# A two-block transformer kernel: token-major products take 512 weight columns at a time instead of 256

## The reference, cut to what matters

```python
h = rms_norm(x, mix_norm_g)
proj = h @ w_in                       # 512 x 1024 times 1024 x 5888
z_a, q, k, v, gate_logits = jnp.split(proj, [1536, 2304, 3072, 3840], axis=-1)
y_a = chunked_spatial_gating(gelu(z_a), ...)   # u = columns 0..767, v-part = 768..1535
...
y_b = dilated_mixture_attention(q, k, v)       # v: 3 groups of 4 heads x 64 = 3 x 256 columns
```

## Time and profile before

| | |
|---|---|
| median of 3 runs | 1986.85 us |
| the profiled execution | 1987.81 us, of which the span of the trace 1986.0 us |
| TensorE matmuls busy | 1874.4 us, 94% of the span, 9685 instructions |
| TensorE weight loads busy | 1373.3 us, 69%, 9691 instructions |
| VectorE, ScalarE, GpSimd busy | 983.6 us, 657.0 us, 85.3 us |
| mean granted TensorE clock | 0.977 of full speed |

### The profile page before, as it was taken

How to read it: one execution, slowest core, us unless ns; L and a number is a source line. 1 busy time by engine, 2 the same in 40 slices (tenths; PEclk the granted TensorE clock), 3 DMA queues, 4 the chain that set the end, 5 groups by cost and what they waited for, 6 DMA issues and landing times.

```text
span 1986.0 us, 23349 instructions
## 1 busy us (share of the span) xinstructions
PE 1874.4 (94%) x9685; PEld 1373.3 (69%) x9691; DVE 983.6 (50%) x1620; ACT 657.0 (33%) x1134; POOL 85.3 (4%) x70
## 2 busy tenths in 40 slices
PE   6989999999999699999999799999898999999998
PEld 4877777788878434344433289898677788888886
DVE  4888877843552422231322254525565556636643
ACT  4445544532332301020110144223545443222333
POOL 0200000000000000000000000002130200000000
PEclk9999999999999799999999999999898999999999
DMA  9332333252343499999999932252211332233221
GB/s 323 120 111 92 121 92 96 88 188 94 104 182 115 152 419 421 421 421 422 420 421 421 395 107 82 89 171 64 64 43 64 129 99 90 75 128 106 66 93 43
DMA packets 176539, 355.13 MB, mean 179 GB/s; under 512 B 7122, under 2 KB 148530, under 8 KB 151090
## 3 DMA queue, kind: packets, MB, share of 16 engines
q1 hardware_dynamic: 172688, 338.85, 46.3%
q10 hardware_dynamic: 3458, 14.50, 2.0%
q0 software_dynamic: 288, 0.30, 0.1%
HBM read 345.53 MB, written 8.39 MB: 178 GB/s over the span
## 4 chain that ended last, share of the span: by engine, by line
PE 77%; DVE 10%; ACT 5%; DMA 4%; issue 2%; POOL 2%; SPq 0%; ACTq 0%; DVEq 0%; POOLq 0%
PE ps L487 74%; PE ps L490 2%; DMA rx<-in_w_exp_up 1%; DMA rx<-in_w_exp_down 1%; DVE small L2122 1%; ACT M L1238 1%; POOL X L2790 1%; DVE wsp0l L1877 1%; DVE wsq1l L1877 1%; DMA md<-in_w_mod 1%; DVE X L1886 1%; DVE k2l L1877 1%; ACT KR L1238 1%; POOL tb L2790 1%; POOL MH L2790 1%
## 5 line engine op out<-in xcount | busy, mean ns | idle before, releaser
L487 PE MATMUL ps<-H,wsq1h 128*128 128x512 f32 x640 | 200.2, 394 | 4.7 <-DVE wsq1l L1877 2.7
L487 PE MATMUL ps<-H,wsq0h 128*128 128x512 f32 x608 | 191.0, 395 | 0.2 <-DVE wsq0l L1877 0.2
L487 PE MATMUL ps<-rx,XE 128*64 128x512 f32 x752 | 176.7, 600 | 2.9 <-DMA rx<-in_w_exp_up 2.2
L487 PE MATMUL ps<-H,wsp1h 128*128 128x512 f32 x544 | 173.8, 401 | 1.4 <-DVE wsp1l L1877 1.4
L487 PEld LDWEIGHTS ps<-H,wsq1h 128*128 128x128 f32 x640 | 119.7, 189 | 30.4 <-issue 6.1
L487 PEld LDWEIGHTS ps<-H,wsq0h 128*128 128x128 f32 x608 | 114.5, 190 | 25.4 <-issue 2.3
L487 PE MATMUL ps<-H,wsq1l 128*128 128x512 f32 x320 | 125.2, 391 | 0.0
L487 PE MATMUL ps<-H,wsp0h 128*128 128x512 f32 x368 | 121.4, 408 | 2.1 <-ACT H L1238 2.1
L1877 DVE TENSOR_TENSOR wsq1l<-ring,wsq1h 128x1024 fp32r<-128x1024 f32 (+2 forms) x72 | 82.9, 1191 | 78.0 <-ACT wsq1h L1238 77.9
L487 PE MATMUL ps<-H,wsq0l 128*128 128x512 f32 x304 | 119.0, 391 | 0.0
L487 PEld LDWEIGHTS ps<-H,wsp1h 128*128 128x128 f32 x544 | 100.6, 192 | 22.2 <-issue 3.5
(11 more groups left out here) (378 smaller groups left out, 3576.0 us busy)
## 6 DMA issues: line engine op xcount, KB each, us to landing
rx<-in_w_exp_gate SPq DMA_DIRECT2D x49, 1024.0 KB, 17.2
rx<-in_w_exp_down SPq DMA_DIRECT2D x46, 1024.0 KB, 20.7
rx<-in_w_exp_up SPq DMA_DIRECT2D x45, 1024.0 KB, 19.4
ring<-in_w_in SPq DMA_DIRECT2D x39, 1024.0 KB, 5.3
ring<-in_w_up SPq DMA_DIRECT2D x20, 1024.0 KB, 5.1
ring<-in_w_exp_up SPq DMA_DIRECT2D x19, 1024.0 KB, 20.6
ring<-in_w_mod SPq DMA_DIRECT2D x18, 1024.0 KB, 6.9
ring<-in_w_exp_down SPq DMA_DIRECT2D x18, 1024.0 KB, 19.3
```

Of the source, the lines that this page charges most:

```text
L487: return pe.e.matmul(o, l, r, start=start, stop=stop, skip_group_check=True)
```

## The change

`lin_n` now works on a pair of slabs, each of 4 chunks of 128 rows by 512 columns (also 1 MB). It goes through the four token tiles with the first slab (h = 0) and again with the second (h = 1), so four banks are open at once, and each is complete, with 512 columns, only in the second round. The 768 columns of `v2` and the 256 columns of the first attention group, 1024 in all, become two such pairs; the second takes its columns from two places in `w_in_2`, so each of its slabs is loaded by two transfers. The 512 columns of attention groups 2 and 3 become one pair `av`, with tokens r, r+4, .... ScalarE empties a bank of the second pair in two steps (gelu into `vg`, scaled copy into `va`), one of `av` in a single 512-column step. `va` moves to a place of its own, since it is now written while `vg` is still wanted, and `vr`, `pT2`, `mk2`, `idb2` and `pp` shift with it. The eight steps of `first_norm` are spread over four slabs instead of three.

```diff
-    for n in range(3):
-        piece(("v2", n), w_in2, 0, 8, 768 + 256 * n)
+    for h in range(2):
+        piece(("v2", 0, h), w_in2, 4 * h, 4, 768, 512)
+    for h in range(2):
+        slab(("v2", 1, h), [(0, 256, rows(w_in2, 4 * h, 4, 1280, 256)), (256, 512, rows(w_in2, 4 * h, 4, 3072, 256))], 4, 512)
...
-    for n in range(3):
-        piece(("av", n), w_in2, 0, 8, 3072 + 256 * n)
+    for h in range(2):
+        piece(("av", 0, h), w_in2, 4 * h, 4, 3328, 512)
...
+        def lin_n(key, hh, hl, toks, frees):
+
+            for h in range(2):
+                s = slabs[key + (h,)]
+                wh, wl = hi_lo(s)
+                for n, cols in enumerate(toks):
+                    if h == 0:
+                        take((key, n), frees(n))
+                    o = bank(where[key, n], 0, s.cols)
+                    for k in range(4):
+                        c = 4 * h + k
+                        pe.wait_ge(S["v_lo"], (s.key, half_of(s, k)))
+                        mm(o, hh[:, c, cols], wh[:, k, :], c == 0, False)
+                        mm(o, hl[:, c, cols], wh[:, k, :], False, False)
+                        i = mm(o, hh[:, c, cols], wl[:, k, :], False, c == 7)
+                    if h:
+                        i.then_inc(*S["pe_group"].tick((key, n)))
+                final[s.key] = (key, len(toks) - 1) if h else (s.key, "used")
+                if h == 0:
+                    i.then_inc(*S["pe_group"].tick((s.key, "used")))
...
-        lin_n(("av", 0), H2h, H2l, [slice(i * P, (i + 1) * P) for i in range(4)], lambda i: [("a_take", (("av", 0), i))])
-        for g in range(2):
-            lin_n(("av", 1 + g), H2h, H2l, [slice(r, T, 4) for r in range(4)], lambda r: [("a_take", (("av", 1 + g), r))])
+        lin_n(("av", 0), H2h, H2l, [slice(r, T, 4) for r in range(4)], lambda r: [("a_take", (("av", 0), r))])
...
-        for n in range(3):
-            ahead(("v2", n))
+        for n in range(2):
+            ahead(("v2", n, 0))
             for i in range(4):
+                if i == 1:
+                    ahead(("v2", n, 1))
+                b, w = where.get((("v2", n), i), 0), 256 if n else 512
                 ac_.wait_ge(S["pe_group"], (("v2", n), i))
...
+                t = act(vgv[:, i, 512 * n:512 * n + w], bank(b, 0, w), ACT.Gelu, scale=r2[:, i:i + 1])
+                if n:
+                    t = act(vav[:, i, :], bank(b, 256, 512), ACT.Copy, scale=r2[:, i:i + 1])
+                t.then_inc(*S["a_take"].tick((("v2", n), i)))
...
-        for n in range(3):
-            ahead(("av", n))
+        for h in range(2):
+            ahead(("av", 0, h))
```

More of the change, by code:

```diff
@@ L297, in emit @@
     k2l = at("k2l", 3072, F32R, sq + 24576)
[L298 to L303, removed]
+    va = at("va", 1024, F32, sq + 35072)
+    pT2 = at("pT2", 1536, F32, sq + 27648)
+    vr = at("vr", 2048, F32, sq + 29184)
+    mk2 = at("mk2", M_END2, BF16, sq + 31232)
+    idb2 = at("idb2", 128, BF16, sq + 31624)
+    pp = [at(f"pp{i}", 1536, F32, sq + 31688 + 1536 * i) for i in range(2)]
     turn_of = [(tb[:, 0:512], tb[:, 512:1024], acc2[:, :].bitcast(F32R)),
@@ L310, in emit @@
     vav = va[:, :].rearrange("p (i n) -> p i n", n=256)
+    vr4 = vr[:, :].rearrange("p (r n) -> p r n", r=4)
     vrv = vr[:, :].rearrange("p (r g n) -> p r g n", r=4, g=2)
@@ L1647, in scalar @@
                 act(ugv[:, 2 * n + m, :], ugv[:, 2 * n + m, :], ACT.Gelu).then_inc(*S["a_take"].tick((("u2", n), m)))
-        for n in range(3):
-            ahead(("v2", n))
+        for n in range(2):
+            ahead(("v2", n, 0))
             for i in range(4):
+                if i == 1:
+                    ahead(("v2", n, 1))
+                b, w = where.get((("v2", n), i), 0), 256 if n else 512
                 ac_.wait_ge(S["pe_group"], (("v2", n), i))
-                act(vgv[:, i, 256 * n:256 * n + 256], bank(where.get((("v2", n), i), 0), 0, 256), ACT.Gelu,
-                    scale=r2[:, i:i + 1]).then_inc(*S["a_take"].tick((("v2", n), i)))
+                t = act(vgv[:, i, 512 * n:512 * n + w], bank(b, 0, w), ACT.Gelu, scale=r2[:, i:i + 1])
+                if n:
+                    t = act(vav[:, i, :], bank(b, 256, 512), ACT.Copy, scale=r2[:, i:i + 1])
+                t.then_inc(*S["a_take"].tick((("v2", n), i)))
         ahead(("g0", 0))
         for i in range(4):
-            ac_.wait_ge(S["a_take"], (("v2", 2), i))
+            ac_.wait_ge(S["a_take"], (("v2", 1), i))
             if i:
@@ L1683, in scalar @@
         free_at = [("pe_group", final.get(("b0", 3))), ("v_take", (("b0", 3), 1)), ("m_out", "m")]
-        for n in range(3):
-            ahead(("av", n))
[L1686 to L1692, removed]
+        for h in range(2):
+            ahead(("av", 0, h))
+        for i in range(4):
+            ac_.wait_ge(S["pe_group"], (("av", 0), i))
+            for signal, key in free_at:
+                ac_.wait_ge(S[signal], key)
+            ac_.wait_ge(S["v_norm"], "r2s")
+            act(vr4[:, i, :], bank(where.get((("av", 0), i), 0)), ACT.Copy, scale=r2s[:, i:i + 1]).then_inc(
+                *S["a_take"].tick((("av", 0), i)))
         def rope_hi(jj, g, m):
@@ L2492, in vector @@
         cp(wsT[:, :], bank(where.get("ws", 0))).then_inc(*S["v_gmlp"].tick("wsT"))
[L2493 to L2496, removed]
+        for n in range(2):
+            for h in range(2):
+                ahead(("v2", n, h))
+                for i in range(3):
+                    next(normed, None)
         ahead(("g0", 0))
```

## The result

The changed kernel took 1968.32 us (median of 4 runs, 1966.39 to 1971.0) beside 1987.09 us for the kernel before (4 runs, 1986.59 to 1987.64): a ratio of 0.9907, 95% interval 0.9895 to 0.9919. That is 18.8 us less where 25.0 were forecast; 1962 was forecast and 1957 to 1972 given as the range. The profiled execution took 1966.39 us, 21.4 less than the profiled one of before.

What follows compares the result with a forecast made beforehand. TensorE was taken to bound the kernel, with strided weight loads pacing av 1 and 2. 90.95 us would become 43.52 + 22.40 = 65.92, -25.0, so 1986.85 becomes 1962 us; own range 1958 to 1966, with most of rival 3 1957 to 1972.

Steps and rivals of the forecast that it cites:

- v2 with the first values: Stages v2 and av 0: 192 matmuls of 512 columns at 0.2267 us, 46.15 us to 43.52, a gain of 2.6.
- av: Values of groups 2 and 3: 96 matmuls at the strided load's pace of 0.233 us, 44.80 us to 22.4.
- rivals 1 and 2: At av, strided loads hide only in part (0.42 us a matmul, 7%) or don't overlap at all (0.556 us, 3%).
- rival 2: At av's 96 pairs: the strided load doesn't overlap at all, 0.556 us each, 1993 us in total; chance 3%.
- The stride: At av 1 and 2: strided weight loads set the pace, 0.233 us against 0.120 in order, for 256 columns.
- What must stay hidden: From v2 on: splits, bank emptying and transfers stay behind TensorE's shorter slabs, 10.88 us in v2, 11.2 in av.
- The slack at av's second slab: VectorE's low part, behind the wait for M2's spill, would be ready about 2 us before TensorE wants it.
- Rival 3: At av's second slab: late spill, 2 us stall, then lower clock costing up to 3.3 us; 1967 us, chance 10%.
- Behind av everything moves as a block: From qk on: same slabs and banks, old distances kept, so no time gained or lost there.
- Rival 4: In the attention: something TensorE doesn't drive gates it, so the gain is given back; 1987 us, chance 2%.
- the prediction's own signs of being wrong: Av's pace above 0.25 us; low-part waits at av's second slab or g0 0; more time from qk to the end.

Runs made afterwards that it cites:

- the count put back: Changed kernel with the running count of bank turns moved up by 8 behind av, so wo2 starts in its old banks: 1963.07 us, ratio 0.9882.
- turns shifted: Kernel before with the count of bank turns moved down by 8 behind av, so wo2 starts in banks 5 and 6: 1992.39 us, ratio 1.0028.
- av alone: Kernel before with only groups 2 and 3's values as a 512-column pair, wo2's old banks kept: 1966.49 us, ratio 0.9899.

## Why the prediction was right, and where it wasn't

- *v2 with the first values*: 34.64 + 11.51 = 46.15 us became 43.67; forecast 43.52. Right: 43.67 / 192 = 0.2274 us a matmul, without a wait.
- *av*: 44.80 us became 22.56; forecast 22.4. The pace is 22.56 / 96 = 0.235 us, that of the scores' rows. PEld is busy nearly throughout (22.52 of 22.56 us, against 36.13 of 43.67 in v2), and the pace lies by 0.008 above that of in-order loads. So the load seems still to set the pace, by that little, and otherwise runs beside the 512 columns. This refutes rivals 1 and 2 (0.42 and 0.556 us), and with rival 2 the Trainium skill's rule in "Part 3: Packing small matmuls", page "TensorE: Matmul & The Clock Gate", at least for this kind of load. (The same part also has a load pulled ahead when it goes to the background weight buffer, which would allow what is seen here.)
- *The stride*: that the load and not the columns bound av 1 and 2 was read from two paces; the runs with other strides show it, as there only the stationary operand's addresses change and the pace goes from 0.120 to 0.242 us. The Trainium skill, "Advanced Engine Details and Errata", section "SBUF Cachelines", has lines of 16 bytes, of which each needs at least two hits for full speed; strides 2 (two hits) and 4 (one) agree with it, at 0.120 and 0.233 us.
- *What must stay hidden*: g0 to b0 is unchanged at 82.2 us, and qk to the first scores at 43.9. g0 0's low part was made from 1220.94 to 1223.30, 3.8 us before TensorE wanted it at 1227.08, as worked out. The slack at av's second slab was smaller than the 2 us forecast. ScalarE and VectorE there:

```profile
1310.21 0.33 ACTq L1268 DMA_DIRECT2D m_spill<-M  x1
...
1318.46 0.23 DVE L1901 CAST idb<-cst 128x128 bf16<-128x128 f32 x1 [8.29 <-DMA m_spill<-M]
1318.60 2.35 DVE L1889 TENSOR_TENSOR wsq1l<-ring,wsq1h 128x1024 fp32r<-128x1024 f32 x2
```

The spill landed 8.3 us after its issue instead of 6.9, 9.2 after av's start instead of 7.85. The first half of the low part was through at about 1319.8 and TensorE began the slab at 1320.56: some 0.7 us were left. Rival 3 in its first part (late low part) was that near, and didn't happen; its second part, a stretch at the lower clock behind a wait, came behind another wait.
- *The step that failed* is in the sentence "Behind av everything moves as a block: same slabs, same banks for qk (26 and 34 bank turns are both even)". It is true for qk and its list of two banks, and I stopped there. Two lists later, at wo2, the same count is taken modulo 7. In the sum this wait stood at nothing. What the runs show in its place is a wait of 6.0 us, with or without the 512-column products, and without it once the count is put back. Rival 4 asked for something in the attention that TensorE doesn't drive, and looked in the wrong stage. One of the prediction's own signs of being wrong came true: from qk to the end the profiled execution takes 632.8 us, the one before 627.5.
- *The luck in it*: 1968.32 us lies outside the forecast's own range, 1958 to 1966. It lies inside 1957 to 1972 only because the range was widened for rival 3, a late low part, and that didn't happen. A loss of about the same size from another place fell into the room made for it.
- *The clock*: behind that wait the matmuls start 0.51 to 0.42 us apart for 2.7 us, and then 0.23. The granted clock over the 10 us is 0.85, a mean of its two levels (1.2 and 2.4 GHz), where TensorE had idled 6 us just ahead; in the kernel before, without that idle time, the 10 us from wo2's start are at 1.00. First the changed kernel, then the one before:

```profile
1541.39:1551.39 10.00, 10.00 (x38) 8.16 (x39) 3.38 (x3) 2.65 (x4) 3.40 (x3) 0.85 0.56 205
...
1562.02:1572.02 10.00, 9.97 (x44) 7.82 (x43) 7.06 (x9) 3.17 (x5) 9.61 (x6) 1.00 0.00 0
```

With the count put back, the ratio 0.9882 (0.9868 to 0.9895) on 1985.47 us is 20.8 to 26.2 us, with 23.4 in the middle; the forecast of 25.0 lies in it, and the profiled executions of that kernel and of the one before are 24.3 apart (24.1 from v2's start to the end). The forecast's sum was therefore good for what it counted, and the measured 18.8 is that sum less the wait it hadn't counted, give or take what varies between executions. Why the changed kernel's runs spread (1964.8 to 1971.0 over both chips) and those of the kernel with the count put back lie within 0.65 us stays open; four runs are few, and the kernel before spreads by 6.4 us on one chip.

## What to carry to other kernels

When a product takes fewer banks, follow the rotation of banks to the end of the program and redo it for each list and its length: a product that begins in the bank which is emptied last waits for the whole emptying, however far away the edit was. When tokens are the stationary operand, make the moving one as wide as the bank, above all where the load is strided: at stride 4 a matmul took 0.235 us with 512 columns and 0.233 with 256, so the second half of the columns was nearly free. Where a pace changes inside one stage with nothing else different, look at the record of the load beside it before blaming the matmul.

## What the runs showed of the hardware

With a 128-column float32 stationary operand, 256-column products go at 0.120 us for strides 1 and 2, 0.176 for 3, 0.233 for 4, 0.226 for 5 and 0.242 for 8, all at a granted clock of 1.00. Of the theories tried, only a cost by the number of 16-byte stretches touched, up to one per column, fits all but the last few per cent.

The transfer of `M2` to memory behind b0 (`m_spill`, 2 MB) took 6.9 to 7.0 us to land in the five profiled executions whose v2 has the old slabs (before, turns shifted, av alone, strides 2 and 3, strides 5 and 8), and 7.8 to 8.2 us in the three with the new ones. It took two thirds of the 2 us of slack at av's second slab. More traffic beside it is not the reason: from its issue to its landing the core's DMA engines moved 353 GB/s in 6.96 us before and 300 GB/s in 8.19 us after, about 2.46 MB both times, and were busy for 0.93 and 0.79 of the time. No run was made to find the cause, and it stays open:

```profile
1303.14:1310.10 6.96, 6.96 (x60) 6.96 (x59) 0.03 (x1) 2.01 (x2) 0.00 (x0) 1.00 0.93 353
...
1310.21:1318.40 8.19, 8.19 (x36) 8.19 (x36) 0.00 (x0) 2.01 (x2) 0.00 (x0) 1.00 0.79 300
```
